# Stick-breaking attention weights on one Trainium2 core: the weighted sum of values taken by parts

## What is computed

```python
def stick_breaking_attention(q, k, v):
    ...
    for start in range(0, S, Q_BLOCK):          # Q_BLOCK = 128
        end = start + Q_BLOCK
        qb, kb, vb = q[:, start:end], k[:, :end], v[:, :end]
        z = jnp.einsum('bqhd,bkhd->bhqk', qb, kb).astype(jnp.float32) * scale
        t_idx = start + jnp.arange(Q_BLOCK)[:, None]
        s_idx = jnp.arange(end)[None, :]
        strict = s_idx < t_idx
        log_beta = jax.nn.log_sigmoid(z)
        log_1m_beta = jnp.where(strict, jax.nn.log_sigmoid(-z), 0.0)
        suffix = lax.cumsum(log_1m_beta, axis=3, reverse=True) - log_1m_beta
        w = jnp.where(strict, jnp.exp(log_beta + suffix), 0.0)
        outs.append(jnp.einsum('bhqk,bkhd->bqhd', w.astype(v.dtype), vb))
```

## Time and profile before

| what | value |
|---|---|
| median of 3 runs | 1019.44 us (1017.79 to 1019.54) |
| profiled execution, its own time | 1019.48 us |
| its span | 1017.7 us |
| TensorE matmuls busy | 983.9 us, 97% of the span |
| VectorE busy | 667.8 us, 66% |
| ScalarE busy | 492.9 us, 48% |
| GpSimd busy | 89.1 us, 9% |
| mean granted TensorE clock | 0.995 of full speed |

### The profile page before, as it was taken

One profiled execution on the slowest core, in us unless ns is written; L12 is line 12 of the kernel. 1 busy time (PEld: TensorE's weight loads), 2 busy tenths in 40 slices (PEclk: granted clock), 3 DMA queues, 4 the chain that ended last, 5 costly groups with the idle time before them and its releaser, 6 DMA issues.

```text
span 1017.7 us, 13127 instructions
## 1 busy us (share of the span) xinstructions
PE 983.9 (97%) x4784; PEld 817.4 (80%) x4784; DVE 667.8 (66%) x1230; ACT 492.9 (48%) x989; POOL 89.1 (9%) x200
## 2 busy tenths in 40 slices
PE   9999999999999999999998879999999999999998
PEld 7888988888888888777886757798888888888886
DVE  6387778868788758467678986977444454445453
ACT  6357687743323445589777663434224214313420
POOL 1001001011112011000004331100000000000000
PEclk9999999999999999999999998999999999999999
DMA  8123131248788515342332224426413223232221
GB/s 299 67 105 94 63 106 52 84 161 306 286 300 301 181 76 150 110 131 76 94 104 63 63 63 157 175 83 123 171 59 124 84 83 124 92 116 83 83 72 53
DMA packets 29247, 127.65 MB, mean 125 GB/s; under 512 B 4600, under 2 KB 4600, under 8 KB 19584
## 3 DMA queue, kind: packets, MB, share of 16 engines
q1 hardware_dynamic: 18704, 96.10, 27.9%
q0 software_dynamic: 7408, 26.75, 7.4%
q10 hardware_dynamic: 3072, 3.98, 1.1%
HBM read 118.40 MB, written 4.22 MB: 120 GB/s over the span
## 4 chain that ended last, share of the span: by engine, by line
PE 81%; DVE 11%; ACT 4%; issue 3%; POOL 1%; DMA 0%; ACTq 0%; POOLq 0%; DVEq 0%; SPq 0%
PE psum L1761 24%; PE psum L1763 24%; PE psum L1762 24%; DVE sgt L1210 2%; PE psum L1913 2%; PE psum L1892 2%; DVE wl L1014 1%; PE psum L1933 1%; DVE ptl L1227 1%; PE psum L1935 1%; DVE two L1543 1%; DVE p_sb L1218 1%; PE psum L1786 1%; DVE tmp L1522 1%; DVE two L1413 1%
## 5 line engine op out<-in xcount | busy, mean ns | idle before, releaser
L1761 PE MATMUL psum<-hh,wh 128*128 128x512 f32 (+1 forms) x720 | 276.4, 384 | 0.0
L1763 PE MATMUL psum<-hh,wl 128*128 128x512 f32 (+1 forms) x720 | 267.9, 372 | 0.0
L1762 PE MATMUL psum<-hl,wh 128*128 128x512 f32 (+1 forms) x720 | 267.7, 372 | 0.0
L524 ACT ACTIVATE wh<-raw 128x512 fp32r<-128x512 f32 x292 | 169.5, 620 | 132.6 <-PE psum L1763 118.9
L1014 DVE TENSOR_TENSOR wl<-raw,wh 128x512 fp32r<-128x512 f32 x292 | 192.7, 685 | 17.8 <-ACT wh L524 17.3
L1763 PEld LDWEIGHTS psum<-hh,wl 128*128 128x128 f32 x720 | 135.4, 188 | 23.8
L1761 PEld LDWEIGHTS psum<-hh,wh 128*128 128x128 f32 x720 | 135.7, 189 | 21.2 <-issue 1.0
L1762 PEld LDWEIGHTS psum<-hl,wh 128*128 128x128 f32 x720 | 135.9, 189 | 19.1 <-issue 0.7
L1761 PE MATMUL psum<-wh,ah 128*128 128x512 f32 x320 | 126.3, 395 | 1.8 <-ACT sgt L668 1.8
L1763 PE MATMUL psum<-wh,al 128*128 128x512 f32 x320 | 125.1, 391 | 0.0
L1762 PE MATMUL psum<-wl,ah 128*128 128x512 f32 x320 | 125.1, 391 | 0.0
(11 more groups left out here) (260 smaller groups left out, 1511.2 us busy)
## 6 DMA issues: line engine op xcount, KB each, us to landing
raw<-in_wall SPq DMA_DIRECT2D x75, 1024.0 KB, 5.0
wa<-in_wada POOLq DMA_DIRECT2D x20, 512.0 KB, 5.7
gt<-in_wada POOLq DMA_DIRECT2D x20, 512.0 KB, 6.7
wb<-in_wada POOLq DMA_DIRECT2D x8, 512.0 KB, 7.4
xt<-in_xcols SPq DMA_DIRECT2D x8, 264.0 KB, 7.8
cb<-c_rows SPq DMA_DIRECT2D x8, 264.0 KB, 3.3
x<-in_x SPq DMA_DIRECT2D x4, 512.0 KB, 8.1
x_kept<-x SPq DMA_DIRECT2D x4, 512.0 KB, 2.8
```

The costliest lines, as they stand in the source:

```text
L524: e.activation(home(w)[0][:, 512 * c:512 * c + 512], raw_of(w, c), ACT.Copy).then_inc(a["wh"], 1)
L1761: e.matmul(out_, lh, rh, start=start, stop=False, skip_group_check=True)
L1762: e.matmul(out_, lh, rl, start=False, stop=False, skip_group_check=True)
L1763: return e.matmul(out_, ll, rh, start=False, stop=stop, skip_group_check=True)
```

## The change

Writing w(s) = P(s+1) - P(s) and moving the difference from the weights to the values gives, for query t,

out(t) = v(t) + sum over s <= t of P(s) (v(s-1) - v(s)), with P(t) = 1 and v(-1) = 0.

- ScalarE computes only sigmoid(-z), into the weight buffer (`sigmoid`).
- VectorE scans it in place, from its end, with state = state * sigmoid(-z) + strip (age 2). The strip is zero but for an identity in its last 128 columns: right of the diagonal the state stays zero, on the diagonal it becomes 1, left of it it is the running product. So there is no mask, and no product with a second buffer.
- The scores' banks come free with that one sigmoid.
- TensorE adds v(t) to the output bank before a head's first value product: four 128 x 128 transposes of the raw values, in transpose mode, accumulated by the products that follow.
- The values: ScalarE copies a block raw to new rows (with 64 zero columns beside each head's values), SyncE's queue moves it one row down in the buffer `dv` by DMA (127 rows of 4 pieces of 256 bytes, for odd and even heads apart; from the second block on also the last row of the block before, as a DMA of one row), VectorE subtracts (steps 84, 85, 97, 105), ScalarE copies the upper half (steps 85, 86, 98, 106) and VectorE makes the lower half (steps 86, 87, 99, 107).
- GpSimd writes the zeros and the strip before head 16.

```diff
-AGE = dict(..., sig=1, scan=3, weight=4, ph=1, ...)
+AGE = dict(..., sig=1, scan=2, ph=1, ...)
...
+        DV, DV_UPPER, DV_LOWER = (84, 85, 97, 105), (85, 86, 98, 106), (86, 87, 99, 107)
...
+            def values_before(i):                                   # SyncE
+                e.wait_ge(a["vsb"], i + 1)
+                if i == 2:
+                    e.wait_ge(v["vsb"], 1)
+                elif i == 3:
+                    e.wait_ge(v["score"], n_score(14, 0))
+                for odd in range(2):
+                    e.dma_start(heads_of(dv[i])[1:128, :, odd, :],
+                                values_at(i)[0:127, :, odd, :]).then_inc(d[f"dv{i % 2}"], 16)
+                    if i:
+                        e.dma_start(heads_of(dv[i])[0:1, :, odd, :],
+                                    values_at(i - 1)[127:128, :, odd, :]).then_inc(d[f"dv{i % 2}"], 16)
...
+                if m in (5, 6):
+                    values_before(m - 3)
                 loads_to(W_CA + m + 1 + NR)
+                if m == 4:
+                    ...
+                    values_before(0)
+                    values_before(1)
...
-            def sigmoids(h, i):                                     # ScalarE
-                ...
-                e.activation(block_p(h, i), scores_at(h, i), ACT.Sigmoid).then_inc(a["sig"], 1)
-                if n_sb(h, i) > 2:
-                    e.wait_ge(v["pw"], n_sb(h, i) - 2)
-                ...
-                e.activation(gg[:, 512 - n:512], scores_at(h, i), ACT.Sigmoid, scale=-1.0).then_inc(a["sig1"], 1)
+            def sigmoid(h, i):
+                ...
+                e.activation(block_p(h, i), scores_at(h, i), ACT.Sigmoid, scale=-1.0).then_inc(a["sig"], 1)
...
-                e.wait_ge(g["mask1"], 2 * n_sb(h, i))               # VectorE, sticks
-                e.tensor_tensor_scan(gg[:, ::-1], gg[:, ::-1], ones[:, 0:1].to_broadcast([128, n]), 1.0, ALU.mult,
-                                     ALU.mult).then_inc(v["scan_s"], 1)
-
-            def stick_weights(h, i):
-                ...
+                p, ends_at = block_p(h, i), strip[:, 512 - n:512]
+                e.wait_ge(a["sig"], n_sb(h, i))
+                ...
+                e.tensor_tensor_scan(p[:, ::-1], p[:, ::-1], ends_at[:, ::-1], 0.0, ALU.mult,
+                                     ALU.add).then_inc(v["scan_s"], 1)
...
-                if n in VSB_OUT:                                    # VectorE, values
-                    i = VSB_OUT.index(n)
+                if n in DV:
+                    i = DV.index(n)
                     e.wait_ge(a["vsb"], i + 1)
-                    e.tensor_tensor(v_sb[:, i, :, 64:128], bank[VSB_BANK[i]]..., v_sb[:, i, :, 0:64]..., ALU.subtract)...
+                    e.wait_ge(d[f"dv{i % 2}"], (32, 64, 96, 128)[i])
+                    ...
+                    e.tensor_tensor(heads_of(dv[i]), heads_of(dv[i]), values_at(i), ALU.subtract).then_inc(v["dv"], 1)
+                if n in DV_LOWER:
+                    ...
...
-            def mask_sb(h, i):                                      # GpSimd
-                ...
+            for i in range(4):
+                e.memset(v_rows[i][:, :, 64:128], 0.0).then_inc(g["strip"], 1)
+            e.memset(strip[:, 0:384], 0.0).then_inc(g["strip"], 1)
+            e.tensor_scalar(strip[:, 384:512], ident[:, :], 1.0, None, ALU.mult).then_inc(g["strip"], 1)
...
-                    e.wait_ge(a["sig1"], c - 66)                    # TensorE, score
+                    e.wait_ge(a["sig"], c - 66)
...
-                    e.wait_ge(v["pw"], n_sb(h, i0))                 # TensorE, turn
+                    e.wait_ge(v["scan_s"], n_sb(h, i0))
...
+                    if h in SB:                                     # TensorE, value, before block 3
+                        ...
+                        for i in range(4):
+                            e.matmul(out_bank(h)[:, 128 * i:128 * i + 128], values_at(i, h), ident[:, :],
+                                     start=(i == 0), stop=False, is_transpose=True, skip_group_check=True)
```

More of the change, by code:

```diff
@@ L85, in pieces_of @@
     return out
-AGE = dict(logits=1, max=2, exp=3, rcp=4, norm=5, sig=1, scan=3, weight=4, ph=1, pl=2, half=1, both=2, oh=3, ol=4,
+AGE = dict(logits=1, max=2, exp=3, rcp=4, norm=5, sig=1, scan=2, ph=1, pl=2, half=1, both=2, oh=3, ol=4,
            gate=3, oh_fg=4, ol_fg=5)
@@ L160, in program @@
         low_2 = sb("low_2", [128, 1056], F32R)
+        br = ExitStack()
+        rows = sb("rows", [128, 5128], where=br)
+        br.close()
         gt = sb("gt", [128, 2, D])
@@ L226, in program @@
         k_2 = sb("k_sb2", [128, 2, SEQ], F32R, where=b2)
+        v_end = sb("v_end", [128, 768], where=b2)
         b2.close()
         bt = (sgt[:, 0:512], sgt[:, 512:1024])
-        gb = (sgt[:, 1024:1537], sgt[:, 1538:2051])
         sq = two
+        v_rows = [y_.rearrange("p (a b) -> p a b", a=4)
+                  for y_ in (rows[:, 3072:3840], rows[:, 3840:4608], v_end[:, :], rows[:, 1024:1792])]
+        strip = rows[:, 4608:5120]
+        dv = (x1[:, 3, 0:512], x1[:, 3, 512:1024], x1[:, 3, 0:512], sgt[:, 0:512])
         w2 = ExitStack()
@@ L710, in beat @@
                 if (x_ := at(AGE["sig"])) and x_[0] == "S" and x_[1] in SB:
-                    sigmoids(*x_[1:])
+                    sigmoid(*x_[1:])
                 if (x_ := at(AGE["ph"])) and x_[0] == "T":
@@ L1738, in _ @@
                 if h == 9:
+                    for j in range(4):
+                        e.wait_ge(d[f"x{4 + j}"], 32)
+                    e.memset(dv[0][0:1, :], 0.0).then_inc(g["strip"], 1)
                     gate_rows()
                     gate(0)
-            for x_ in beats_s:
-                if x_ and x_[0] == "S" and x_[1] in SB:
-                    mask_sb(*x_[1:])
+            e.wait_ge(v["qn"], 8)
+            e.wait_ge(v["tile"], 40)
+            for i in range(4):
+                e.memset(v_rows[i][:, :, 64:128], 0.0).then_inc(g["strip"], 1)
+            e.memset(strip[:, 0:384], 0.0).then_inc(g["strip"], 1)
+            e.tensor_scalar(strip[:, 384:512], ident[:, :], 1.0, None, ALU.mult).then_inc(g["strip"], 1)
             e.wait_ge(t["value"], n_turn(23, 0))
@@ L1928, in value @@
                     if h == 17:
[L1929 removed]
+                        e.wait_ge(a["vsb"], 3)
                     elif h:
                         e.wait_ge(v["o"], h if h < 17 else h - 1)
+                    if h in SB:
+                        if h == 16:
+                            e.wait_ge(g["strip"], 5)
+                        for i in range(4):
+                            e.matmul(out_bank(h)[:, 128 * i:128 * i + 128], values_at(i, h), ident[:, :],
+                                     start=(i == 0), stop=False, is_transpose=True, skip_group_check=True)
                 e.wait_ge(v["turn"], n_turn(h, j))
[L1933 removed]
+                e.matmul(out_bank(h)[:, 128 * i0:512], lhs, ph[:, PT[j]:PT[j] + w_], start=(j == 3 and h not in SB), stop=False,
                          skip_group_check=True)
```

64 lines of the change are left out of this document (32 added, 32 removed).

## The result

| | before | after |
|---|---|---|
| median | 1019.40 us (4 runs, 1017.79 to 1019.54) | 1058.22 us (4 runs, 1057.70 to 1058.69) |
| span of the profiled execution | 1017.7 us | 1055.5 us |
| mean granted clock | 0.995 | 0.977 |

A forecast was written before the change was run, and what follows sets the result against it. TensorE was taken as the bound, idle only between 535 and 625 us (14.54 us). Stalls 35.6 + 13.4 + 7 and clock 7 sum to 63, less the stage's 11.7: +51.3 us, 1071 us; range 1005 to 1094 us.

The forecast's parts named there:

- One engine for 127 rows: Values' DMAs: 127 is prime, so each gets one DMA engine, not sixteen; chance 0.62.
- The rivals with sixteen engines: Values' DMAs on sixteen engines: hidden, 1009 us, chance 0.28; with a dearer step, 1013 to 1018 us, chance 0.10.
- The price of a packet: Values' DMAs: 18 ns per 256-byte packet, middle of 12 and 24; 9.1 us per DMA, 18.3 per block.
- The stalls: TensorE held via VectorE's waits for values' DMAs: 35.6 us for blocks 0 and 1, 13.4 for block 2, 7 for block 3.
- The clock: TensorE returns at half clock after the three long stalls for the values: 7 us lost.
- The cover: Slack of 2.3 us between L1227 (lower half of transposed weights) at 498.70 and the value product at 501.00.
- The stage: Sweep of heads 16 to 23, 535 to 625 us: -11.7 us in sum, -6.5 with dearer transposes.
- the score and product waits and the last sigmoid's: Stage: transposes awaiting a product and scores awaiting the second sigmoid, 1.4 us; a matmul awaiting the last second sigmoid, 2.1 us.
- the own values: Stage: 32 added TensorE transposes cost 0.44 us per four, 3.5 us for eight heads; 8.7 us at full row time.
- The stage gains nothing (rival): ScalarE's chain from the previous output sets every head; either case about 4 us later, 1075 or 1013 us.
- the dearer scan: Stage: scan reading a strip could cost the products' 16.1 us more; forecast took no change from 26.7 us.
- The rival with a dearer step: Sixteen engines, but transposes at 0.27 us or VectorE held 3 to 6 us over the cover: 1013 to 1018 us; chance 0.10.

The follow-up runs named there:

- experiment 1: The changed kernel with each DMA of 127 rows cut into one of 112 and one of 15 rows: 1012.66 us, ratio 0.9932 to the kernel before.
- experiment 2: The changed kernel with each DMA of 127 rows cut into 96 and 31 rows: 1016.31 us, ratio 0.9976 to the kernel before.
- experiment 3: The changed kernel without the DMAs that move the values or VectorE's wait for them, values subtracted from themselves: 1008.67 us, ratio 0.99 to the kernel before.
- experiment 9: The kernel of experiment 8 plus one VectorE product per block behind the scan, which the transposes wait for: 1019.11 us, stage 92.94 us.
- experiment 10: The kernel of experiment 8 plus a second, unread sigmoid of each block on ScalarE before the one the scan takes: 1013.51 us, stage 86.40 us.
- experiment 8: The kernel of experiment 1 with blocks 0 and 1 issued ahead of the weight load and subtractions at steps 86, 87, 97, 110: 1008.00 us, ratio 0.9897.
- experiment 7: The kernel of experiment 1 with the own values' transposes issued twice, 64 instead of 32: 1014.53 us, ratio 0.996, stage 83.68 us.

## Why the prediction was right, and its size off by 13 us

1057 to 1059 us were measured, 1071 predicted, in the range and on the side forecast. The range, 1005 to 1094 us, spans both signs and says little; what the prediction had right is the side, to which it gave 0.62, and the steps below.

- **One engine for 127 rows: right**, by one completion packet per DMA, and by experiments 1 and 2. The rivals with sixteen engines gave 1009 to 1018 us; cut in two by experiment 1, the DMAs bring the kernel there (1012.66).
- **The price of a packet: too high**, and the term that was mis-sized. I took 18 ns, the middle of 12 and 24; it is 14.5. A packet's own time is 17.9 ns by the same working as the earlier trace rows, so the middle hit that, by luck; what failed is to lay 508 such times end to end, when the packets start 14.0 to 14.5 ns apart. Block 1 was forecast for 535.1 us and its wait ended at 525.2. Four DMAs at 7.4 instead of 9.1 us are 7 of these 10 us. The rest is the start: I let them begin at 497, when the load has landed, but their packets already run while it lands (139 small ones between 495 and 497.3 us, at most 16 of them the load's completions).
- **The stalls: right in mechanism, too large.** Forecast 35.6, 13.4 and 7 us; measured 25.4, 9.0 and 7.4, and a last one of 1.2: 43.0 instead of 56. My own sums, 1044 at 12 ns and 1071 at 18, give 1055 at 14.5. Block 3's 7 us came out right by two errors: between 12 and 18 ns its term gives 3.4 at 14.5, but I had its DMAs directly behind block 2's. SyncE issued a 1 MB load between them (546.54 us), and block 3 landed 18.9 us behind block 2, where its 1016 packets take 14.7.
- **The clock: right in mechanism, its size only as a remainder.** The granted clock is 0.50 from 505 to 525 us, with TensorE idle, and 0.66 on average from 525 to 535 us, where it works again. 49.5 us less 43.0 of gaps leaves 6.5, with the 0.8 us of experiment 3 and the gaps' modelled ends in it; forecast 7.
- **The cover: right.** 2.3 us stood between the lower half and the value product. In experiment 1 VectorE is held 2.99 us, and TensorE waits 0.69 us before that product (0.96 us idle from 500 to 510 us in all).
- **The stage: -12.1 us, forecast -11.7; the sum right, the waits right, the shares of the removed instructions not.** Before transposes 2.5 us and four gaps of 0.17 are 3.2 (forecast 3.5); before value products 4.8 and five gaps, 5.7 (6.0); the score and product waits and the last sigmoid's are gone, as forecast (3.5), and the clock stays up (2.2 by the forecast; not measured by itself). These add up to 14.6, so 2.5 are left for the own values: forecast +3.5, by leaving them out 0.5, by doubling them 2.8. As the place of the waits, with everything removed at once, the terms hold; as the price of one removed instruction they do not: experiments 9 and 10 show that the product alone is worth all of the gain and the sigmoid half of it.
- **The stage gains nothing (rival): refuted**, and so is the dearer scan: 816 ns.
- **A sum that does not come out.** The rival with a dearer step was put at 1013 to 1018 us. Its terms, 5.2 or 6 us on the 1019.4 - 11.7, give 1013 and 1014 alone and 1019 together. Nothing measured rests on it.

What stays open: why the gap near 526 us shortens only with both edits of experiment 8; there is one trace of each. And why the product costs 12 us, when its 32 instructions take 15.7 us of a VectorE that was not full: the waits show where, not how each head's lateness comes about.

## What to carry to other kernels

Before a transfer is shifted by one row, count the engines it will get: here 127 rows had one engine and 112 + 15 had 16 and 15, and the second DMA was worth 45 us. Put such transfers ahead of a large load if nobody needs the load yet, and the instruction that waits for them behind, not in front of, the work that TensorE is about to need; here both together were worth some 4 us, and neither is shown to help alone. And price the removal of several operations from one chain by walking the chain once with all of them gone; what one is worth by itself shows only when it is put back, and these prices need not add: here 12.1 and 5.5 us out of 12.1.

## What was not expected of the hardware

- **Issuing blocks when one engine has a backlog.** SyncE spent 17.84 us on three issues, and 7.05 and 6.94 us on DMAs of one row, which take 0.68 to 0.70 us each in experiment 1. The latter are about the 7.4 us of one 508-packet DMA. Everything behind on that queue goes out late, here the next table at 526.74 instead of 502.09 us (experiment 1), though none of TensorE's waits above is for it.
- **One DMA engine moves 256-byte packets at 18 GB/s**, one every 14.0 ns while it is fed (14.5 with the pause), though each takes 17.9 ns. The share of all 16 reads 7.7% meanwhile: a low DMA share is no proof that nobody waits for a DMA.
- **TensorE's time for a 128-column transpose** is 0.28 us by its row (278 ns) and 0.09 us by what one more adds in experiment 7; four in a row move the next matmul by 0.35 us.
